# Moving the tiles of a decoder kernel to multiples of 512 bytes in a partition

## What is computed

```
for layer in range(2):
    h = rmsnorm(x, mix_norm[layer]);  z = h @ w_in[layer]          # 1024 x 4392
    q, k, v, qi, ki, wi, u, ga, gp = split(z)
    a = dsa_attention(rope(norm(q)), rope(norm(k)), v, qi, ki, wi)  # each query keeps 64 keys
    p = pool_mixer(u, w_pool[layer], pool_scale[layer])
    merged = sigmoid(ga) * (a @ w_attn_proj[layer]) + sigmoid(gp) * (p @ w_pool_proj[layer])
    x = x + merged @ w_out[layer]
    h2 = rmsnorm(x, ffn_norm[layer])
    if layer == 0:  x = x + (silu(h2 @ w1) * (h2 @ w3)) @ w2        # 1024 -> 2816 -> 1024
    else:           x = x + sum over 8 experts e of                 # 1024 -> 3584 -> 1024, top 2 of 8
                        gate[e] * ((silu(h2 @ w1[e]) * (h2 @ w3[e])) @ w2[e])
```

## Time and profile before

| | |
|---|---|
| median of 3 runs | 1588.71 us (1586.83 to 1590.33) |
| the profiled execution | 1589.16 us, its span 1587.3 us |
| mean granted TensorE clock | 0.988 |
| PE busy, weight loads busy | 1547.0 us, 1270.7 us |
| DVE, ACT busy | 1267.5 us, 1052.3 us |
| moved by DMA | 445.32 MB, mean 281 GB/s |
| expert loop (575 to 1560 us) | PE busy 975.77 of 985 us, DMA 342 GB/s |

### The profile page before, as it was taken

One profiled execution on the slowest core, in us unless ns is written; L12 is line 12 of the kernel. 1 busy time (PEld: TensorE's weight loads), 2 busy tenths in 40 slices (PEclk: granted clock), 3 DMA queues, 4 the chain that ended last, 5 costly groups with the idle time before them and its releaser, 6 DMA issues.

```text
span 1587.3 us, 22532 instructions
## 1 busy us (share of the span) xinstructions
PE 1547.0 (97%) x7253; PEld 1270.7 (80%) x7253; DVE 1267.5 (80%) x1329; ACT 1052.3 (66%) x1159; POOL 5.9 (0%) x12
## 2 busy tenths in 40 slices
PE   7999999999999899999999999999999999999997
PEld 6888888788888778878878878877887887887885
DVE  5885655446976579799789789799889979978978
ACT  6565544336464467687687687687778768768766
POOL 0000000000000000000000000000000000000000
PEclk9999999999999789999999999999999999999998
DMA  9543565358543669799899999999989989989985
GB/s 333 160 162 129 186 202 167 106 190 283 167 160 108 234 228 305 262 367 371 290 379 370 313 362 367 330 340 371 373 299 372 373 292 367 369 296 376 372 296 195
DMA packets 329116, 445.32 MB, mean 281 GB/s; under 512 B 14144, under 2 KB 269160, under 8 KB 329080
## 3 DMA queue, kind: packets, MB, share of 16 engines
q1 hardware_dynamic: 328512, 442.71, 81.8%
q0 software_dynamic: 480, 2.13, 0.4%
q10 hardware_dynamic: 88, 0.02, 0.0%
HBM read 443.76 MB, written 1.05 MB: 280 GB/s over the span
## 4 chain that ended last, share of the span: by engine, by line
PE 83%; DMA 4%; issue 4%; DVE 4%; ACT 3%; SPq 1%; DVEq 0%; ACTq 0%
PE bank L746 26%; PE bank L748 25%; PE bank L747 25%; DMA w_raw<-in_moe_w 4%; PE bank L1034 2%; ACT w_hi L448 2%; PE bank L1060 2%; DVE w_lo L1125 1%; DVE hT_lo L1515 1%; SPq L351 1%; PE bank L828 1%; DMA w_raw<-in_w_in 1%; PE bank L772 1%; ACT hT_hi L737 0%; PE bank L812 0%
## 5 line engine op out<-in xcount | busy, mean ns | idle before, releaser
L1125 DVE TENSOR_TENSOR w_lo<-w_raw,w_hi 128x1024 fp32r<-128x1024 f32 (+1 forms) x448 | 780.7, 1755 | 110.8 <-ACT w_hi L448 110.2
L448 ACT ACTIVATE w_hi<-w_raw 128x1024 fp32r<-128x1024 f32 (+1 forms) x448 | 663.8, 1492 | 157.6 <-PE bank L748 143.8
L746 PE MATMUL bank<-w_hi,hT_hi 128*128 128x512 f32 (+1 forms) x1424 | 567.5, 399 | 6.6 <-DVE hT_lo L1515 2.5
L748 PE MATMUL bank<-w_hi,hT_lo 128*128 128x512 f32 (+1 forms) x1424 | 554.9, 390 | 0.0
L747 PE MATMUL bank<-w_lo,hT_hi 128*128 128x512 f32 (+1 forms) x1424 | 553.6, 389 | 0.0
L746 PEld LDWEIGHTS bank<-w_hi,hT_hi 128*128 128x128 f32 x1424 | 268.7, 189 | 62.3 <-issue 6.8
L748 PEld LDWEIGHTS bank<-w_hi,hT_lo 128*128 128x128 f32 x1424 | 268.5, 189 | 56.6
L747 PEld LDWEIGHTS bank<-w_lo,hT_hi 128*128 128x128 f32 x1424 | 269.2, 189 | 50.8
L1120 DVE TENSOR_TENSOR w_lo<-w_raw,w_hi 128x2048 fp32r<-128x2048 f32 (+2 forms) x100 | 201.5, 2019 | 95.6 <-ACT w_hi L442 94.8
L442 ACT ACTIVATE w_hi<-w_raw 128x2048 fp32r<-128x2048 f32 (+2 forms) x100 | 169.6, 1699 | 160.1 <-PE bank L748 158.6
L746 PE MATMUL bank<-w_hi,hiddenM_hi 128*128 128x512 f32 x448 | 178.7, 399 | 1.1
(11 more groups left out here) (230 smaller groups left out, 1022.9 us busy)
## 6 DMA issues: line engine op xcount, KB each, us to landing
w_raw<-in_moe_w SPq DMA_DIRECT2D x672, 512.0 KB
w_raw<-in_w_in SPq DMA_DIRECT2D x64, 512.0 KB
w_raw<-in_dense_w SPq DMA_DIRECT2D x44, 512.0 KB
w_raw<-in_dense_w SPq DMA_DIRECT2D x44, 256.0 KB
w_raw<-in_w_out SPq DMA_DIRECT2D x16, 512.0 KB
w_raw<-in_w_pool_proj SPq DMA_DIRECT2D x8, 512.0 KB
w_raw<-in_w_attn_proj SPq DMA_DIRECT2D x8, 512.0 KB
w_raw<-in_w_in SPq DMA_DIRECT2D x8, 296.0 KB
```

Source lines behind the costliest of these rows:

```text
L448: act.activation(whi[:, m % SLOTS, 0:n], raw8[m % 8][:, 0:n], ACT.Copy).then_inc(s_hi, 1)
L746: pe.matmul(dst, ahi, bhi, start=start, stop=False)
L748: return pe.matmul(dst, alo, bhi, start=False, stop=stop)
L1125: dve.tensor_tensor(wlo[:, m % SLOTS, 0:n], raw8[m % 8][:, 0:n], whi[:, m % SLOTS, 0:n], ALU.subtract).then_inc(s_lo, 1)
```

## The change

The seven small tiles that live through the whole kernel (4736 bytes in a partition together) are placed first, then an unused tile of 256 bytes, and then the large ones. No instruction is added, removed or moved on any engine; only addresses change, and the line numbers below by one (L448 becomes L449, and so on).

```diff
-        raw = sb("w_raw", [P, SLOTS, FULL])
-        whi = sb("w_hi", [P, SLOTS, FULL], FR)
-        wlo = sb("w_lo", [P, SLOTS, FULL], FR)
-        X = sb("x_residual", [P, TT, D])
-        hThi = sb("hT_hi", [P, KC, S], FR)
-        hTlo = sb("hT_lo", [P, KC, S], FR)
         cst = sb("shape_constants", [P, C_END])
         pcol = sb("param_columns", [P, 40])
         gain = sb("qk_gain", [P, 2, 2, HD])
...
         wrhi = sb("w_router_hi", [P, KC, E], FR)
         wrlo = sb("w_router_lo", [P, KC, E], FR)
+        sb("align_512", [P, 64])
+        raw = sb("w_raw", [P, SLOTS, FULL])
+        whi = sb("w_hi", [P, SLOTS, FULL], FR)
+        wlo = sb("w_lo", [P, SLOTS, FULL], FR)
+        X = sb("x_residual", [P, TT, D])
+        hThi = sb("hT_hi", [P, KC, S], FR)
+        hTlo = sb("hT_lo", [P, KC, S], FR)
         ident = cst[:, C_ID:C_ID + P]
```

## The result

| | before | changed |
|---|---|---|
| median | 1589.48 us (6 runs, 1586.83 to 1590.33) | 1577.67 us (6 runs, 1576.91 to 1578.64) |
| profiled execution, its span | 1589.16, 1587.3 us | 1577.69, 1575.9 us |
| ratio | | 0.9927, 95% interval 0.9914 to 0.9940 |

The account below looks back on a forecast made before the run. PE was taken to bound the kernel, so only its idle time could be gained: 4.6 us from faster up-chunk loads and 0 from everything else, 1588.71 - 4.6 = 1584.1 us, range 1580.8 to 1588.8 us.

Parts of the forecast that it names:

- What bounds the kernel, and the loads' rate: PE bounds; up chunks into w_raw slots 0 to 3 load at 348 GB/s, slots 4 to 7 at 384, from their start.
- the boundary's waits: At seven job boundaries ACT waits for chunks 2 and 6, delaying PE's first transposes; ACT's first wait was to shrink.
- The further 256 bytes: Slots 0 to 3 begin better aligned than slots 4 to 7 did; no trace row, priced at the same fast rate.
- The price of the loads: Faster up chunks shorten PE's waits at seven expert job boundaries: 4.6 us gain, between 3.8 and 5.3.
- The seven waits: PE's first transposes of a job waiting for DVE's product: from 7.0 us to about 2.4 us.
- Down chunks, mixer and dense loads, splits, 0: Loads of down chunks, mixer and dense part, and ACT's and DVE's splits of weights, gain or lose nothing.
- Products: I take 0: Starts 0.227 us apart with hT, 0.232 with hiddenM, laid to the PSUM bank change; no gain or loss.
- The rival that took the fact seriously: Left operand's own place sets the pace; moving hT slows its 4272 products by 21 us, 1610 us; chance 0.07.
- the mirror image: The expert down-products speed up to 0.227 us: 6.7 us on top of 4.6, 1577.4 us; shares chance 0.09.
- loads still faster than forecast: Up loads beat today's slots 4 to 7, removing 7.9 us of PE waits: 1580.8 us; shares chance 0.09.
- The range: Whole kernel: 1580.8 us, all 7.9 us of waits gone, to 1588.8 us, no gain.

Follow-up runs that it names:

- e1: Changed kernel with slots 0 to 3 of w_raw alone back at 128 bytes past a multiple of 512: 1584.81 us, ratio 0.9967.
- e12: Kernel before with slots 0 to 3 of w_raw alone moved to a multiple of 256: 1583.84 us, ratio 0.9965.
- e11: Changed kernel with w_raw at 64 past 256, hidden at distance 160 and hiddenM at 224 from w_hi and w_lo: 1591.33 us, one run.
- e4: Changed kernel with the unused tile 512 bytes long, so all large tiles stand at 256 past 512, distances kept: 1577.02 us, ratio 0.9919.
- e2: Changed kernel with the down-projections' left operands (hiddenM, hidden) moved 128 bytes on: 1585.63 us, ratio 0.9966.
- e6: Changed kernel with distances from w_hi and w_lo, modulo 256, of 32 (hidden), 64 (hiddenM), 0 (pT, aT): 1585.23 us, ratio 0.9972.
- e7: Changed kernel with distances from w_hi and w_lo, modulo 256, of 96 (hidden), 192 (hiddenM), 32 (pT, aT): 1581.42 us, ratio 0.9941.
- e3: Changed kernel with the down-projections' left operands (hiddenM, hidden) moved 256 bytes on: 1577.77 us, ratio 0.9922.
- e8: Changed kernel with w_hi and w_lo moved 128 bytes on, all left operands left in place: 1601.65 us, ratio 1.0064.

## Why the prediction was wrong

*What bounds the kernel, and the loads' rate.* Right. The alternation of 348 and 384 GB/s was the 128 bytes (e1, e12; 64 bytes do the same, e11), all of `w_raw`'s slots came to 385, and the boundary's waits went as described. The further 256 bytes gave nothing (e4).

*The price of the loads, 4.6 us (3.8 to 5.3).* Right: 5.6 (3.8 to 7.3) alone in e12, 5.2 by the stretches of the two traces. The seven waits were forecast at about 2.4 us and came to 2.1 in e12, 1.2 in the changed kernel.

*Down chunks, mixer and dense loads, splits, 0.* Nothing in the traces contradicts it. Down chunks come at 421 and 422 GB/s in the changed kernel (880 to 886 us). DVE's rest still takes 2.28 us, ACT's split 1.92.

*"Products: I take 0".* This step failed. The rows had the fact, 0.227 us against 0.232, and the working laid the 5 ns to the change of PSUM bank after every three products. The down-projection still changes its bank so, and runs at 0.227 us: the bank was worth nothing, the distance between operands all of it. The rival that took the fact seriously looked only at the left operand's own place, and so gave the slower case, 21 us, a chance of 0.07, while the mirror image shared 0.09 with loads still faster than forecast. The mirror image, "the down-products come to 0.227 us", is what happened. That its 1577.4 us came to within 0.3 us of the median is in part luck. Its working was for `hiddenM` alone, 6.7 us; the eight down-projections gave 5.6 us, in part since PE idled 2.0 us in them beside 1.1 before; `hidden` added 1.4 us, and the mixer, whose operands came from the distance 192 to 64, took some back.

*The range.* Its lower end, 1580.8 us, was the sum of PE's waits. A bound made of idle time holds only if no busy time shrinks, and one of the rivals named in the same text broke it.

What could have been read beforehand: a third family. The mixer's products with pT stood at a third distance, 192 (320 and 128 past 512), and changed their bank only after twelve products, as those with `hT` do in the mixer. Their means in the trace of before are neither 389 nor 394:

```profile
L747 PE MATMUL bank<-w_lo,pT_hi 128*128 128x512 f32 x32 | 12.6, 392 | 0.0
```

So three places gave three paces, and the bank could explain but one of them. It is a hint and no more, since there are only 32 such products.

## What to carry to other kernels

When two groups of the same instruction differ by a few ns in a kernel that one engine fills, list everything in which they differ, addresses included, before one cause gets the difference; here 5 ns in 1608 products, 8.0 us, were as much as all of PE's waits in the expert loop, 7.9 us. Where operands are placed is a part of such a kernel: put left and right operands of products a multiple of 256 bytes apart in a partition, begin the targets of loads with short runs (1024 bytes here) at a multiple of 256, and check it by the starts in the trace. Both were measured only for the products and loads of this kernel. Don't bound a gain by idle time alone when the change could touch the length of the busy instructions.

## What the runs showed of the hardware

- After a product of 128x128 by 512 float32r columns the next starts 0.227 to 0.228 us later if left and right operand stand a multiple of 256 bytes apart in the partition, and 0.229 to 0.234 us if they don't (means over the three products of a split; seven other distances tried, all multiples of 32, e2, e6, e7, e11). Neither operand's own place counted (e3, e4, e8).
- Loads in runs of 1024 bytes, with the queue full: 385 GB/s to places at a multiple of 256 (e4, e12), 349 at 64 past one (e11) and 348 or 349 at 128 past one (e1). Runs of 4096 bytes at 128 past one showed no loss, 423 GB/s beside 420.
- The Trainium skill (SBUF — State Buffer, "Operand start alignment") says of its rules on where an operand may begin that they are "about legality, not speed". In this case a start of its own cost a product nothing, but the distance of two operands did, and so did the start of a load's target; both have their numbers above.
- With PE faster in the down-projections, its waits at the job boundaries were longer: 8.8 us in e1 beside 7.0 before, at the same rates of loads, 349 and 385 GB/s beside 349 and 384 (one trace each).
